# Inner inverses of 16x16 on VectorE in place of 8x8 ones and one TensorE level, in a hybrid decoder step

## The reference

```python
def step(S, inp):
    r_t, w_t, k_t, v_t, a_t, b_t = inp
    sa = jnp.einsum('bhij,bhj->bhi', S, a_t)
    S = S * w_t[..., None, :] + sa[..., :, None] * b_t[..., None, :] + v_t[..., :, None] * k_t[..., None, :]
    o = jnp.einsum('bhij,bhj->bhi', S, r_t)
    return S, o
```

## Time and profile before

| | us |
|---|---|
| median of three runs | 1237.55 |
| lowest, highest | 1235.53, 1238.72 |
| the profiled execution, its time | 1237.24 |
| its span in the profile | 1235.7 |
| TensorE busy | 1194.3 (97%) |
| VectorE busy | 734.8 (59%) |
| ScalarE busy | 535.5 (43%) |
| GpSimd busy | 237.8 (19%) |
| granted TensorE clock, mean | 0.994 |

### The profile page before, as it was taken

How to read it: one execution, slowest core, us unless ns; L and a number is a source line. 1 busy time by engine, 2 the same in 40 slices (tenths; PEclk the granted TensorE clock), 3 DMA queues, 4 the chain that set the end, 5 groups by cost and what they waited for, 6 DMA issues and landing times.

```text
span 1235.7 us, 21976 instructions
## 1 busy us (share of the span) xinstructions
PE 1194.3 (97%) x8060; PEld 1146.9 (93%) x8060; DVE 734.8 (59%) x1237; ACT 535.5 (43%) x862; POOL 237.8 (19%) x347
## 2 busy tenths in 40 slices
PE   4999999999999999999997999999999999999996
PEld 4889999999999999999997899999999999979996
DVE  5858585958677585858569444444344354475441
ACT  5244464637364554626362233333333343344431
POOL 3233141405032231403054100000000400001111
PEclk9999999999999999999999999999999999999998
DMA  9714334333424333342364355555555964415650
GB/s 229 188 51 118 108 85 112 92 102 94 113 77 131 94 97 111 80 119 78 104 169 115 101 167 145 148 153 145 147 145 158 265 172 137 136 52 155 172 145 21
DMA packets 275418, 155.37 MB, mean 126 GB/s; under 512 B 7717, under 2 KB 270541, under 8 KB 274724
## 3 DMA queue, kind: packets, MB, share of 16 engines
q1 hardware_dynamic: 266896, 137.03, 39.9%
q0 software_dynamic: 8336, 17.79, 5.7%
q10 hardware_dynamic: 148, 0.04, 0.0%
HBM read 149.45 MB, written 5.61 MB: 125 GB/s over the span
## 4 chain that ended last, share of the span: by engine, by line
PE 91%; DVE 5%; ACT 2%; issue 1%; DMA 1%; SPq 0%; POOL 0%; POOLq 0%; DVEq 0%; ACTq 0%
PE acc L1516 19%; PE acc L1517 18%; PE acc L1518 18%; PE wide L1518 5%; PE wide L1517 5%; PE wide L1516 5%; PE wide L1535 2%; PE wide L1682 2%; PE wide L1675 2%; DVE wl L1019 2%; PE wide L1605 1%; PE wide L1885 1%; PE wide L1642 1%; DVE win_a L1343 1%; PE wide L1648 1%
## 5 line engine op out<-in xcount | busy, mean ns | idle before, releaser
L1019 DVE TENSOR_TENSOR wl<-wraw,wh 128x1024 fp32r<-128x1024 f32 x256 | 318.7, 1250 | 225.5 <-ACT wh L685 218.0
L685 ACT CAST wh<-wraw 128x1024 fp32r<-128x1024 f32 x256 | 266.7, 1047 | 251.8 <-PE acc L1518 155.2
L1516 PE MATMUL acc<-hh,wh 128*128 128x320 f32 (+1 forms) x1084 | 362.8, 335 | 7.0 <-DVE wl L1019 7.0
L1517 PE MATMUL acc<-hl,wh 128*128 128x320 f32 (+1 forms) x1084 | 337.3, 311 | 0.0
L1518 PE MATMUL acc<-hh,wl 128*128 128x320 f32 (+1 forms) x1084 | 336.8, 311 | 0.0
L1516 PEld LDWEIGHTS acc<-hh,wh 128*128 128x128 f32 x1084 | 205.3, 189 | 11.2 <-issue 7.7
L1517 PEld LDWEIGHTS acc<-hl,wh 128*128 128x128 f32 x1084 | 205.1, 189 | 3.4
L1518 PEld LDWEIGHTS acc<-hh,wl 128*128 128x128 f32 x1084 | 204.5, 189 | 0.0
L1516 PE MATMUL acc<-x1h,wh 128*128 128x320 f32 x256 | 82.6, 323 | 0.4 <-DVE x1l L1473 0.4
L1516 PE MATMUL acc<-mh,wh 128*128 128x320 f32 x256 | 80.5, 315 | 0.0
L1518 PE MATMUL acc<-x1h,wl 128*128 128x320 f32 x256 | 79.1, 309 | 0.0
(11 more groups left out here) (364 smaller groups left out, 2250.8 us busy)
## 6 DMA issues: line engine op xcount, KB each, us to landing
wraw<-in_w_in SPq DMA_DIRECT2D x160, 512.0 KB, 3.8
wraw<-in_w_branch SPq DMA_DIRECT2D x32, 512.0 KB, 4.0
wraw<-in_w_out SPq DMA_DIRECT2D x32, 512.0 KB, 4.0
wraw<-in_w_ple_gate SPq DMA_DIRECT2D x32, 512.0 KB, 4.0
xt<-in_x_prompt SPq DMA_DIRECT2D x2, 1024.0 KB, 7.1
S0n<-in_state_wkv POOLq DMA_DIRECT2D x64, 32.0 KB, 4.4
out<-so POOLq DMA_DIRECT2D x16, 128.0 KB, 2.8
xt<-in_x_prompt POOLq DMA_DIRECT2D x2, 1024.0 KB, 7.3
```

The lines of the kernel that those rows point to most:

```text
L685: A.copy(wh[:, slot, :], wraw[:, slot, :]).then_inc(s["hi_ready"], 1)
L1019: V.tensor_tensor(wl[:, slot, :], wraw[:, slot, :], wh[:, slot, :].bitcast(F32), ALU.subtract).then_inc(s["lo_ready"], 1)
L1516: M.matmul(out[:, 0:width], wh[:, slot, wcol], hi, start=first, stop=False)
L1517: M.matmul(out[:, 0:width], wh[:, slot, wcol], lo, start=False, stop=False)
```

## The change

The inner inverse on VectorE goes on from 8x8 to 16x16 blocks, in 16 compact columns per chunk: 24 more counted steps on `base_step` (47 in place of 23), among them sixteen more row shuffles, two products of 320 elements and two reductions of 320 and 360. The first level on TensorE is gone (LEVELS 2 in place of 3). `AKBD` and `ARK` move from the inner inverse into the levels' waits, behind a new semaphore `akb_ready`. Both key transposes stand in one burst between the first products and the first update and go to banks 4 and 5. Their copies on ScalarE move behind `go(4)`, `go(5)` and `out(2)`, and the tails wait for them (`keys_ready`). On VectorE `go(3)`, `out(1)` and `go(4)` stand inside the inner inverse, `go(5)` and `go(6)` behind the levels' masks, `out(2)` in the first level, and `out(3)` at g = 0 of the chain. On TensorE 27 steps follow the scores, the mean has 3 behind it in place of 4, and at the end of a pass 2 are left in place of 7. The pieces that are left out below are constants' tables, buffers' places, a split of the embedding weights and names of semaphores.

```diff
-LEVELS = 3
+LEVELS = 2
 OCT = 8
+HEX = 16
...
-BASE_STEPS = 23
+BASE_STEPS = 47
...
-    put(CF, f, "octs", (row // OCT)[:, None] == np.arange(C // OCT)[None])
+    put(CF, f, "octs", (row // HEX)[:, None] == np.arange(C // HEX)[None])
+    put(CF, f, "upper8", (row % HEX < OCT) * 1.0)
+    put(CF, f, "lower8", (row % HEX >= OCT) * 1.0)
 
     m = np.zeros((P, N_CM), np.float32)
...
-    put(CM, m, "inner", (s // OCT == t // OCT) & (s < t) & seq)
+    put(CM, m, "inner", (s // HEX == t // HEX) & (s < t) & seq)
     a = CM["level"][0]
     for n in range(LEVELS):
-        m[:, a + n * TP:a + (n + 1) * TP] = level(OCT * 2 ** n).reshape(P, TP)
+        m[:, a + n * TP:a + (n + 1) * TP] = level(HEX * 2 ** n).reshape(P, TP)
 
     def diagonal(x):
         x = np.broadcast_to(x, (P, G, C))[:, :, None, :] & (head[:, None, None, None] == np.arange(2)[None, None, :, None])
...
         assert scratch.next <= used["rn"][1]
+        scratch = Region(used["pm"][0])
+        parts8 = scratch.take("parts8", [P, G, OCT + 1, OCT])
+        oct_in = scratch.take("oct_in", [P, G, OCT])
+        cross16 = scratch.take("cross16", [P, G, OCT])
+        half16 = scratch.take("half16", [P, G, OCT])
+        sixteen = scratch.take("sixteen", [P, G, HEX])
+        assert scratch.next <= used["aS"][1]
+        rows8 = at(used["kkn"][0], "rows8", [P, G, OCT, OCT])
...
+                go(4)
+                go(5)
+                out(2)
                 act.wait_ge(s["bt_ps"], r + 1)
-                A.copy(BtBD[:, :, :, :].rearrange("p g h c -> p (g h c)"), B45[:, 0:2 * TP])
-
-                act.wait_ge(s["kt_ps"], r + 1)
-                A.copy(KtBD[:, :, :, :].rearrange("p g h c -> p (g h c)"), B23[:, 0:2 * TP])
-                for n in range(LEVELS):
-                    go(4 + n)
-                out(2)
-                go(4 + LEVELS)
+                A.copy(BtBD[:, :, :, :].rearrange("p g h c -> p (g h c)"), B[4][:, :]).then_inc(s["keys_ready"], 1)
+                A.copy(KtBD[:, :, :, :].rearrange("p g h c -> p (g h c)"), B[5][:, :]).then_inc(s["keys_ready"], 1)
+                go(6)
+                go(7)
                 act.wait_ge(s["y_ready"], r * (LEVELS + 1) + LEVELS + 1)
...
@@ -1189,62 +1202,85 @@
                     dve.wait_ge(s["base_step"], r * BASE_STEPS + (n + 1))
 
                 stepped(1)
-                V.tensor_reduce(inner[:, :, :], Tm[:, :, :].rearrange("p g (o e) -> p g e o", e=OCT), mybir.AxisListType.X, ALU.add
+                V.tensor_reduce(inner[:, :, :], Tm[:, :, :].rearrange("p g (o e) -> p g e o", e=HEX), mybir.AxisListType.X, ALU.add
                                 ).then_inc(s["base_step"], 1)
                 V.tensor_tensor(ARB[:, :, :], sb[:, :, 1, :], cms("incl").rearrange("p (g c) -> p g c", g=G), ALU.mult)
                 stepped(2)
+                V.scalar_tensor_tensor(oct_in[:, :, :], inner[:, :, OCT:HEX], cfs("lower8"), inner[:, :, 0:OCT], ALU.mult, ALU.add
+                                       ).then_inc(s["base_step"], 1)
+                V.tensor_scalar(cross16[:, :, :], inner[:, :, OCT:HEX], cfs("upper8"), None, ALU.mult).then_inc(s["base_step"], 1)
+                stepped(3)
                 diag = terms[:, :, 0, :]
-                V.scalar_tensor_tensor(diag, inner[:, :, 4:8], cfs("lowers"), inner[:, :, 0:4], ALU.mult, ALU.add
+                V.scalar_tensor_tensor(diag, oct_in[:, :, 4:8], cfs("lowers"), oct_in[:, :, 0:4], ALU.mult, ALU.add
                                        ).then_inc(s["base_step"], 1)
-                stepped(3)
-                V.tensor_scalar(cross[:, :, :], inner[:, :, 4:8], cfs("upper"), None, ALU.mult).then_inc(s["base_step"], 1)
+                stepped(5)
+                V.tensor_scalar(cross[:, :, :], oct_in[:, :, 4:8], cfs("upper"), None, ALU.mult).then_inc(s["base_step"], 1)
                 for k in range(2):
                     V.stream_shuffle(rows2[:, :, k, :], diag, quad_row(k + 1)).then_inc(s["base_step"], 1)
-                stepped(6)
+                stepped(8)
                 V.tensor_tensor(terms[:, :, 2:4, :], terms[:, :, 0, 1:3].unsqueeze(3).to_broadcast([P, G, 2, 4]),
                                 rows2[:, :, :, :], ALU.mult).then_inc(s["base_step"], 1)
-                dve.wait_ge(s["score_ps"], r * 3 + 2)
-                V.tensor_tensor(AKBD[:, :, :, :], sk[:, :, 0, :].unsqueeze(2).to_broadcast(bd),
-                                cms("strict").rearrange("p (g h c) -> p g h c", g=G, h=2), ALU.mult)
-                stepped(7)
-                V.tensor_tensor(terms[:, :, 4, :], terms[:, :, 2, 2:3].to_broadcast([P, G, 4]), rows2[:, :, 1, :], ALU.mult
-                                ).then_inc(s["base_step"], 1)
-                V.tensor_tensor(ARK[:, :, :], sk[:, :, 1, :], cms("incl").rearrange("p (g c) -> p g c", g=G), ALU.mult)
-                stepped(8)
-                V.tensor_reduce(quad[:, :, :], terms[:, :, :, :].rearrange("p g k j -> p g j k"), mybir.AxisListType.X, ALU.add
-                                ).then_inc(s["base_step"], 1)
                 dve.wait_ge(s["score_ps"], r * 3 + 3)
                 V.tensor_tensor(ABD[:, :, :, :], B[4][:, 0:T].rearrange("p (g c) -> p g c", g=G).unsqueeze(2).to_broadcast(bd),
                                 cms("lower").rearrange("p (g h c) -> p g h c", g=G, h=2), ALU.mult
                                 ).then_inc(s["ark_ready"], 1)
-                go(3)
                 stepped(9)
+                V.tensor_tensor(terms[:, :, 4, :], terms[:, :, 2, 2:3].to_broadcast([P, G, 4]), rows2[:, :, 1, :], ALU.mult
+                                ).then_inc(s["base_step"], 1)
+                stepped(10)
+                V.tensor_reduce(quad[:, :, :], terms[:, :, :, :].rearrange("p g k j -> p g j k"), mybir.AxisListType.X, ALU.add
+                                ).then_inc(s["base_step"], 1)
+                stepped(11)
                 V.tensor_scalar(octo[:, :, 0:4], quad[:, :, :], cfs("upper"), None, ALU.mult).then_inc(s["base_step"], 1)
                 for k in range(4):
                     V.stream_shuffle(rows4[:, :, k, :], quad[:, :, :], oct_row(4 + k)).then_inc(s["base_step"], 1)
                 V.tensor_scalar(parts[:, :, 4, :], quad[:, :, :], cfs("lowers"), None, ALU.mult).then_inc(s["base_step"], 1)
-                stepped(14)
+                stepped(16)
                 V.tensor_tensor(parts[:, :, 0:4, :], cross[:, :, :].unsqueeze(3).to_broadcast([P, G, 4, 4]), rows4[:, :, :, :],
                                 ALU.mult).then_inc(s["base_step"], 1)
-                stepped(16)
+                stepped(18)
                 V.tensor_reduce(half_way[:, :, :], parts[:, :, 0:4, :].rearrange("p g k j -> p g j k"), mybir.AxisListType.X,
                                 ALU.add).then_inc(s["base_step"], 1)
-                stepped(17)
+                go(3)
+                stepped(19)
                 dve.sem_inc(s["waits"], 1)
                 for k in range(4):
                     V.stream_shuffle(rows4b[:, :, k, :], half_way[:, :, :], oct_row(k)).then_inc(s["base_step"], 1)
-                stepped(21)
+                stepped(23)
                 V.tensor_tensor(parts[:, :, 0:4, :], octo[:, :, 0:4].unsqueeze(3).to_broadcast([P, G, 4, 4]), rows4b[:, :, :, :],
                                 ALU.mult).then_inc(s["base_step"], 1)
-                stepped(22)
+                stepped(24)
                 V.tensor_reduce(octo[:, :, 4:8], parts[:, :, :, :].rearrange("p g k j -> p g j k"), mybir.AxisListType.X,
                                 ALU.add).then_inc(s["base_step"], 1)
-                stepped(23)
-                V.tensor_tensor(Y[:, :, :].rearrange("p g (o e) -> p g o e", e=OCT),
-                                octo[:, :, :].unsqueeze(2).to_broadcast([P, G, C // OCT, OCT]),
-                                cfs("octs").unsqueeze(1).unsqueeze(3).to_broadcast([P, G, C // OCT, OCT]), ALU.mult
+                out(1)
+                stepped(25)
+                dve.sem_inc(s["waits"], 1)
+                for k in range(OCT):
+                    V.stream_shuffle(rows8[:, :, k, :], octo[:, :, :], hex_row(OCT + k)).then_inc(s["base_step"], 1)
+                V.tensor_scalar(sixteen[:, :, 0:OCT], octo[:, :, :], cfs("upper8"), None, ALU.mult).then_inc(s["base_step"], 1)
+                V.tensor_scalar(parts8[:, :, OCT, :], octo[:, :, :], cfs("lower8"), None, ALU.mult).then_inc(s["base_step"], 1)
+                stepped(33)
+                V.tensor_tensor(parts8[:, :, 0:OCT, :], cross16[:, :, :].unsqueeze(3).to_broadcast([P, G, OCT, OCT]),
+                                rows8[:, :, :, :], ALU.mult).then_inc(s["base_step"], 1)
+                stepped(36)
+                V.tensor_reduce(half16[:, :, :], parts8[:, :, 0:OCT, :].rearrange("p g k j -> p g j k"), mybir.AxisListType.X,
+                                ALU.add).then_inc(s["base_step"], 1)
+                go(4)
+                stepped(37)
+                dve.sem_inc(s["waits"], 1)
```

(55 more changed lines are left out.)

16 lines of the change are left out of this document (9 added, 7 removed).

## The result

The median of 20 runs of the changed kernel is 1239.32 us (1237.0 to 1242.52), that of 20 runs of the kernel before 1237.29 us. The ratio is 1.002 with a 95% interval of 1.0012 to 1.0028: slower by 1.5 to 3.5 us, which is less than the 0.3% (3.7 us) that the prediction took for no change. The profiled execution took 1238.65 us (span 1237.1, against 1237.24 and 1235.7 before); the prediction's sum for it was 1238.3.

A forecast was written before the change was run, and what follows sets the result against it. TensorE bounds the loop when its operands are ready. 8 x (4.5 - 3.73) = +6.2, 7 x -0.69 = -4.8 and -0.3 make +1.1 on the profiled 1237.24 us, 1238.3; forecast median 1238.7, range 1230 to 1247 (8 in 10).

The forecast's parts named there:

- likeliest case: The forecast case for the whole kernel: 1236 to 1241 us, chance 0.42.
- part 3: Mean to next pair's first state matmul: other engines' chain binds, 0.69 us won, about 2.1 per pair become PE waiting.
- part 2: First state matmul to first product: VectorE's longer work makes Y 0.44 us late, the stretch 4.5 us longer per pair.
- part 1: First product towards the mean: to the tails 12.44 us before, 8.71 after, 3.73 less, as one level goes.
- S: Start of the masked Tm on VectorE, 305.39 before the change, from which the prediction counts to the start of Y.
- The forecast gain of 2.4 us a pass: PE's own work per pass: 1.77 us for the level's blocks, 0.5 for waits, about 0.1 for the merged key burst.
- (a): Y is in time for the first product, new small operations at their lower ends: 1234.6 us; chance 0.14.
- (b): The chain behind the mean does not bind, PE keeps its saving: 1230 to 1231 us with half returned; chance 0.16.
- (c): Y is later than thought at the first product: 1243 to 1247 us for 0.5 to 1 us more; chance 0.24.
- (d): The drain rule holds for VectorE's added operations, sixteen shuffles and the rest: +13, 1251 us; chance 0.03.
- the term for the end: Behind the last pair, the chain that follows the mean releases the pooled rows' transposes: 0.3 us less.

The follow-up runs named there:

- e7: Kernel before with masks in the levels' waits and key transposes in one burst, three levels and old inner inverse kept; 1233.37 us, ratio 0.9961.
- e2: Changed kernel without its second group of eight row shuffles, so VectorE's chain to Y is shorter; 1234.01 us, ratio 0.9975.
- e3: Changed kernel with one stream step, not two, behind each U product, four more left for the pair's end; 1224.59 us, ratio 0.9893 (again: 1224.98, 0.9906).
- e5: Changed kernel with ScalarE reading key scale and biases straight from the parameter table, not from GpSimd's copy cur_m; 1226.9 us, ratio 0.9919.
- e4: Kernel before with one stream step, not two, behind each U product, as control of e3; 1238.76 us, ratio 1.0012.
- e9: Kernel before with ScalarE reading scale and biases straight from the parameter table, as control of e5; 1235.88 us, ratio 0.9987.
- e8: Kernel before with one level left out and nothing in its place, its five steps put ahead of the first product; 1219.82 us, ratio 0.9851.
- e1: Changed kernel with six stream steps given back: 21 behind the scores, four behind the mean, seven at the pair's end; 1254.53 us, ratio 1.0149.
- e11: Changed kernel with the second half of the first early gate tile ahead of the pooled rows' transposes behind the last pair; 1239.13 us, ratio 1.0014.
- e10: Changed kernel with the edits of e3 and e5 together and 28 steps behind the scores in place of 27; 1229.01 us, ratio 0.9926.

## Why the prediction was right

**The forecast.** 1238.7 with 1230 to 1247, chances mostly for no change: 1239.3 came, by the mechanism of the likeliest case. In the medians the change is +2.0 us (1.5 to 3.5 by the interval of the ratio) for +1.1 forecast; the two profiled executions differ by +1.4, and the rest these traces don't place. The sum has three parts that nearly cancel, and each was measured:

| stretch | forecast | measured |
|---|---|---|
| M to Z (part 3) | -0.69 | -0.82 |
| Z to P (part 2) | +4.41 | +4.44 |
| P to M (part 1, with 0.1 for the late block) | -3.63 | -3.50 |
| pass | +0.09 | +0.10 |

That a pass comes out within 0.01 is partly luck: P to M is 0.13 short of its forecast, and M to Z makes up for it with 0.13 more.

**Part 1** said 8.71 + 0.1 from first product to tails; it is 8.95 (320.08 to 329.03). The level, the split's absence before `Tm` and the updates without a wait came as forecast. The mis-sized term is the key burst: 0.75 was taken between 0.70 and 0.86, and it takes 0.87 (322.40 to 323.27), so two returns less save nothing here. e7 shows the same number. `go(5)`, `out(2)`, `out(3)` and the key copies cost nothing, as said.

**Part 2** said `Y` starts at S + 13.96; it starts at S + 13.85 (305.68 to 319.53). Shuffles stand 0.115 apart as estimated, and the three wide reductions take 0.70, 0.80 and 0.87, with 0.73 for the first and 1.5 for the two others as the estimate, 0.17 too little. The 27 steps end by slots at 319.63 and the product starts at 320.08, which is 0.45 late against a forecast of 0.44; e2, where `Y` is in time, has the stretch 0.46 shorter. The trace writes 0.29 as idle because the last matmul runs to 319.79; whoever forecasts in slots must add some 0.16 to what the row in brackets says. The rule weighed there, that an operation can't issue before the one ahead of it has drained, as the Trainium skill has it ("VectorE: DVE Perf Modes", section "The DRAIN you can't avoid"), would have made it a full 0.19 to 0.21 for each of the sixteen. The trace does not agree: shuffles of that length start 0.115 apart. The same section says that a next operation which isn't held starts earlier; the prediction's rule left that out, and with that sentence the trace agrees.

**Part 3** said M to L1634 becomes 17.94, M to the state matmul 22.76; they are 17.86 and 22.63. The mis-sized term is what the change gives the chain: 0.34 was read from the idle time ahead of `go(11)`, and L783 starts 0.45 earlier behind the mean than L772 did (10.28 for 10.73). The waits, by slots, are about 0.64 (0.48 in the row) for 0.9 forecast and 1.26 (1.10) for 1.2. `go(11)` is without idle and L783 still waits 3.42 us for `cur_m`. e3 and e5 from two sides show that this chain, and not PE's stream, sets the stretch: four steps more in it cost nothing, a shorter chain shortens it by 1.54. e4 and e9 show that neither holds for the kernel before.

**The forecast gain of 2.4 us a pass in PE's own work** was there: e8 has 2.05 of it, the level with its wait (1.77 + 0.25 forecast), and e7 0.48. One of the two waits of 0.25 is in both, so that they show about 2.3 together. In the changed kernel it went where the text put it.

**The rivals.** (a) and (b) would have shown no wait at L1709 or none at L1668 and L1678; all three are there. (c) did not come: the wait is the forecast one. e1 shows a price that its text had not seen: behind a wait of 2.7 us the clock fell too, in seven of eight passes, so that a much later `Y` would have cost more than its lateness, 1.6 us on top in such a pass. (d) fell with the shuffles' rows.

**What failed** is the term for the end, "Behind the last pair the same chain releases the transposes of the pooled rows, 0.3 less". Counted from the last mean they start 0.60 earlier (8.86 for 9.46), but PE stands idle for 1.86 us ahead of them, which the text didn't say, and in this execution the clock fell behind that wait. Engines by stage after the last pair, in the changed kernel, and its timeline of TensorE:

```profile
634.00:636.00 2.00, 2.00 (x12) 2.00 (x13) 0.99 (x1) 2.00 (x2) 2.00 (x7) 0.66 0.40 78
636.00:638.00 2.00, 2.00 (x10) 2.00 (x9) 1.21 (x1) 1.98 (x2) 2.00 (x4) 0.50 1.02 245
```

```profile
633.91 1.33 PE L1579 MATMUL wide<-cf,uS 128*79 128x128 f32 x8 [1.86 <-DVE gp L1052]
...
635.30 0.47 PE L1561 MATMUL acc<-hl,wh 128*128 128x320 f32 x1
635.57 0.47 PE L1562 MATMUL acc<-hh,wl 128*128 128x320 f32 x1
...
639.92 0.98 PE L1579 MATMUL wide<-cf,spt 120*128 120x120 f32 x8
```

At half clock a stream matmul takes 0.27 from start to start in place of 0.15. The transposes of `spt` so come 1.0 us later behind the last mean than before (14.87 for 13.86). From the last mean to the end of the span it is all the same: 612.05 for 612.14, and PE's wait for VectorE's `ytmp` in that stretch shrank from 3.6 to 2.4 us. So the term measured -0.1 here. In e2 and e5, where the clock stayed up, this stretch is 611.7, 0.4 less than before; but it lies between 610.3 and 617.4 in the runs, so a term of this size is not shown either way.

**The profiled total:** +0.7 up to the first mean, seven passes with +0.8, -0.1 behind; +1.4 for +1.1 forecast.

## What to carry to other kernels

Work on the bounding engine that is cover in one stretch is dead weight in another: before counting an instruction removed as time gained, cut the loop at the places where other engines' results are due and write each stretch as the larger of stream and chain. A change that saves on the bounding engine and yields nothing may lack only a redistribution: here one number in the order of the stream turned +0.2% into -1.1%, and the same number did nothing for the kernel before. When a chain is shortened on one engine, see what that sets free on the others and whether they then run over the chain.

## What the runs showed of the hardware

- **The clock can fall behind a single wait, and need not.** Behind waits of 1.86 us (last pair of the changed kernel) and 2.70 to 2.92 (seven of e1's eight passes), and at the end of one of 2.22 (e11), the granted clock averaged 0.50 to 0.69 over two us, which is the level of 1.2 GHz for most of the time, and a stream matmul took 0.27 for 0.15. Behind a wait of 2.73 in e1 and behind those of 1.84 in e2 and e5 it stayed at 1.00, and so it did behind the waits of 0.48 and 1.10 us in each pass. What decides it these runs don't tell.
- **VectorE is slower beside GpSimd.** The bonus product took 0.45 us in e3, with GpSimd idle, and 1.16 in e10 beside GpSimd's products. The scan took 1.53 in e10; in e3 it took 0.82, and there GpSimd's L558 beside it took 1.13 for 0.61. The Trainium skill ("SBUF — State Buffer", section "Who interferes with whom") says that an instruction of VectorE with two inputs in SBUF contends with one of GpSimd that reads SBUF, and that the later one stands still until the other has ended. By that rule, the trace agrees for L1175: GpSimd's L570 ends at 292.46, and 0.34 later L1175 ends.
- **The float32 burst got no cheaper by being merged:** eight transposes took 0.87 us together, and 0.86 in two bursts by the prediction's sum of slots.
